# Forgetting heads' pages: keys turned on VectorE in 32x32 blocks, scores by token groups, values loaded in slices of 32 tokens

## The chip, the cores and the metric

One core of a Trainium2 chip runs the whole program. The metric is the device time in microseconds (us). PE is TensorE, DVE is VectorE, ACT is ScalarE, POOL is GpSimd and SP is SyncE, which issues DMAs. Everything is float32.

## The reference, cut to what matters

The kernel is one layer of a decoder. The change touches one part of it, the forgetting attention of the sample group: 8 sequences (b) of 8 new tokens each, 8 heads of 64 channels, and a paged cache of 2048 past tokens, 16 pages of 128 tokens for each sequence.

```
kv_past = cache_fox_kv[page_table]          # (8, 2048, 2, 8 heads, 64)
c  = cumsum(concat(logf_past, logf_new))    # forgetting: log decay up to each token
s  = q . k / 8  +  c_q  -  c_key            # (b, head, 8 queries, 2048 + 8 keys)
p  = softmax(where(key <= query, s, -inf))
o  = p . v
```

So 128 pages of keys and 128 pages of values (256 KB each) are read, keys must have their channels on the partitions for the score product, and weights must have their tokens there for the value product.

## The kernel before

Each engine has several Python generators ("streams"). Each yields a due time in the units of PLAN (line 143), and weave (line 158) puts the instructions of an engine's streams in the order of their due times. The order is fixed at build time; on the chip each engine takes its instructions in that order and waits on semaphores. The real time of a stretch is what its instructions take. PLAN's stage "fox", 869 to 1275, holds the pages of the forgetting heads. On PE it is interleaved with the gate projections of the prompt (gates_pe, lines 2246 and 2254), in units of 12 or 10 steps; a step is one 128-row product of 304 to 368 columns. A unit needs ScalarE's tanh of the unit before (line 2284) and VectorE's products (lines 2299 to 2305).

paged builds the schedule of the pages and pages_pe, pages_act, pages_dve play it, for this stage and two others. For the forgetting heads, four head pairs j side by side (rows 32j to 32j+16 of the score bank: 2 heads x 8 queries):

- T: a page of keys (128 tokens x 512) is transposed by PE in four 128x128 blocks into PSUM (line 1599), and copied to SBUF by ACT and DVE by turns (lines 1665, 1658). 128 pages.
- S: after each four pages, four products with 16 stationary columns and 512 moving ones (line 1615), one for each pair, side by side in the array. DVE adds the bias (the decay term) and takes the row maximum (line 1702). Group 4 is the 8 new tokens, against the new keys of all sequences (64 columns). Two score banks by turns.
- M: the maximum over the groups (line 1707), then ACT's exponential over 128 x 2112 elements with its row sum (line 1670).
- P: the weights are transposed by PE, four 128x128 blocks at a time, 17 in all (line 1624), and copied by DVE (line 1717).
- V: four parts, of four pages each (the last with the new tokens too), 16 products of 128 columns with 16 stationary ones to a part (line 1635). Then one scaling (line 1731), one transposition O (line 1642) and two copies (line 1735).

P, V and O of sequence b lie between the pages of b+1. Each of the 256 events has one place in the plan, with extra places after the last page.

Keys arrive through SP's queue (foxk_sp, line 1825) into a ring of 6 pages, which PE's transposition frees. Values arrive through ACT's queue (foxv_page_act, line 1858) into 8 places, freed four at a time by a V part. The bias rows are spread over the 16 rows of each pair by POOL's DMAs (foxbias_pool, line 1875), four for each group of four pages, 128 in all. foxprep makes these rows, from PSUM banks 3 to 6.

Of the kernel before, what the change touches and what calls it, by code (L numbers as in the profile page):

```python
# [22 lines left out]
P = 128  # L23
D = 1024
# [77 lines left out]
def make_sample_tables():  # L102

    new_f = np.full((P, NB, SM), NEG)
    pick = np.zeros((P, P))
    for j in range(4):
        for a in range(2):
            for t in range(NS):
                row = 32 * j + NS * a + t
                pick[2 * j + a, row] = 1  # L110
                for b in range(NB):
                    new_f[row, b, b * NS:b * NS + t + 1] = 0
    fox = np.concatenate([new_f.reshape(P, -1), pick], 1)
# [59 lines left out]
def build(nc, I, O, TAB):  # L173

    with ExitStack() as ctx:
# [1574 lines left out]
        NKR, NVR = 6, 8  # L1750
        SF = PAST + P
        s_fox = [take(SF, f0 + 1536 + SF * i) for i in range(2)]
        o_fox = take(P, f0 + 5888)
        stats_f = take(NB * (2 + 5), f0 + 6016)
        biasN = take(SM, f0 + 6080)
        vn_f = take(512, f0 + 6144)
        bias_f = take(1024, f0 + 6656).rearrange("p (g c) -> p g c", g=2)
        pages = [take(512, f0 + a) for a in (0, 512, 1024, 7680, 8192, 8704, 9216, 9728, 10240, 27680, 28192, 34848, 35360, 35872)]
        k_fox, v_fox = pages[0:NKR], pages[NKR:]
        PT_f = take((NPG + 1) * 64, f0 + 10752).rearrange("p (n j c) -> p n j c", j=4, c=16)  # L1760
        biasT = take(PAST, f0 + 11840)
        B_at = X0
        kts_f = [take(2048, a).rearrange("p (j c) -> p j c", j=4) for a in (f0 + 13888, B_at)]
# [3 lines left out]
        tab_f = take(NB * SM + P, C_at)  # L1767
        newadd = tab_f[:, 0:NB * SM].rearrange("p (b c) -> p b c", b=NB)
        pick_head = tab_f[0:HF, NB * SM:]
        ktn_f = take(4 * SM, C_at + 640).rearrange("p (j c) -> p j c", j=4)  # L1770
# [3 lines left out]
        page_in = ring([-(-(NB * NPG - i) // NKR) for i in range(NKR)] + [-(-(NB * NPG // 4 - i) // 3) * 4 for i in range(3)])  # L1774
# [3 lines left out]
        VP = 4  # L1778

# [49 lines left out]
        V_LAST, VK = NB * NPG - 8, 4  # L1829

        def v_place(n):

            if n < V_LAST:
                return v_fox[n % NVR], n - NVR
            if n < V_LAST + VK:
                return k_fox[n - V_LAST], None
            return v_fox[(n - VK) % NVR], n - VK - NVR

        def foxv_page_act(act):
            for n in range(NB * NPG):  # L1840
                if n == 0:
                    yield at("combine")(1) + 0.5
                    act.wait_ge(s_ptab, 16)
                place, before = v_place(n)
                if before is None:
                    yield pg_fox["due_of"][("T", NB - 1, NPG - 1)] + 0.4
                elif before >= 0:
                    yield pg_fox["due_of"][("V", before // NPG, before % NPG // 4)] + 0.1 + V_STEP * (before % 4)
# [3 lines left out]
                if before is None:  # L1852
                    act.wait_ge(*nth(pg_fox, "turned", NB * NPG))
                elif before >= 0:
                    act.wait_ge(*nth(pg_fox, "mixed", before // 4 + 1))
                else:
                    act.wait_ge(cb["second"], 4)
                act.dma_start(place, page_rows(pid, 1)).then_inc(fv_in[n // 4 % 3][0], 16)
# [5 lines left out]
        def foxbias_pool(pool):  # L1864
            pool.wait_ge(fb["rows_act"], 1)
            pool.wait_ge(fb["rows_dve"], 1)
            for q in range(4 * NB):
                b, G = q // 4, q % 4
                if q >= 2:
                    bb, GG = (q - 2) // 4, (q - 2) % 4  # L1870
                    pool.wait_ge(*nth(pg_fox, "drained", bb * 5 + 1 + GG))
                    pool.wait_ge(s_bias[q % 2], 64 * (q // 2))
                for j in range(4):
                    rows = biasT[b * HF + 2 * j:b * HF + 2 * j + 2, 512 * G:512 * (G + 1)]
                    pool.dma_start(bias_f[32 * j:32 * j + 16, q % 2, :],
                                   rows.unsqueeze(1).to_broadcast([2, NS, 512])).then_inc(s_bias[q % 2], 16)

        def fox_turns(b):
            return [dict(blocks=[k_fox[(b * NPG + p) % NKR][:, j * P:(j + 1) * P] for j in range(4)],
                         dst=lambda kt, p=p: kt[:, :, (p % 4) * P:(p % 4 + 1) * P],  # L1880
                         src=lambda bank: bank.rearrange("p (j c) -> p j c", j=4)) for p in range(NPG)]

        def fox_groups(b, kt):
            out = []
            for G in range(NPG // 4):
                mms = [] if kt is None else [(32 * j, 0, 512, qbF[:, j, b, :], kt[:, j, :], True, True) for j in range(4)]
                out.append(dict(turned=4 * (G + 1), first=True, mms=mms, drain=(G * 512, 512, bias_f[:, G % 2, :])))
            out.append(dict(turned=None, first=True, drain=(PAST, SM, newadd[:, b, :]),
                            mms=[(32 * j, 0, SM, qbF[:, j, b, :], ktn_f[:, j, :], True, True) for j in range(4)]))
            return out  # L1890

        def fox_pv(b):
            for p in range(NPG + 1):
                v = v_place(b * NPG + p)[0] if p < NPG else vn_f
                yield [(banks[7][32 * j:32 * j + 16, 0:P], PT_f[:, p, j, :], v[:, j * P:(j + 1) * P], p == 0, p == NPG)
                       for j in range(4)]

        def fox_p_keep(i, bank):
            n = min(4, NPG + 1 - 4 * i)
            v = bank[:, 0:n * P].rearrange("p (n j c) -> p n j c", j=4, c=32)  # L1900
            yield PT_f[:, 4 * i:4 * i + n, :, :], v[:, :, :, 0:16], None

        def fox_add_ready(eng, b, i):
            if i < 4:
                eng.wait_ge(s_bias[i % 2], 64 * ((4 * b + i) // 2 + 1))

        def fox_v_ready(eng, b, i):
            if b == 0 and i == VP - 1:
                eng.wait_ge(fb["vn_in"], 16)
                eng.wait_ge(fb["vn_clear"], 1)  # L1910
            q = b * VP + i
            landed(eng, fv_in[q % 3], 4 * (q // 3 + 1))

        fox_split = [list(range(4 * q, 4 * q + (4 if q < 3 else 5))) for q in range(VP)]
        fox_tail = [("V", q, 4 * (q + 1)) for q in range(VP)] + [("P", q, 2 + q) for q in range(5)] + [("O", 0, 17)]
        pg_fox = paged(fox_turns, fox_groups, P, kts_f, s_fox, NPG + 1, fox_p_keep, fox_pv, fox_split, o_fox, 1, stats_f,
                       pair_out(oTf, 4), fox_tail, PLAN["fox"],
                       dict(turn=banks[2:4], score=banks[4:6], tail=banks[6], o_ps=banks[7][:, 0:P]), add_ready=fox_add_ready, new_at=NPG - 1,
                       tail_step=1.0)

        def foxprep_pe(pe):
# [19 lines left out]
            pe.matmul(banks[7][:, 0:SM], pick_head, biasN[0:HF, :], start=True, stop=True).then_inc(fb["new_spread"], 1)  # L1941

        def foxprep_act(act):
# [3 lines left out]
            act.activation(biasT[0:SM, 1024:2048], psum[0:SM, 5 * 512:7 * 512], ACT.Copy).then_inc(fb["rows_act"], 1)  # L1947
# [32 lines left out]
        def foxprep_dve(dve):  # L1980
# [3 lines left out]
            dve.memset(bias_f, 0.0)  # L1984
            dve.wait_ge(fb["summed"], 1)
            dve.tensor_copy(biasN[0:HF, :], banks[7][0:HF, 0:SM]).then_inc(fb["new_kept"], 1)
            dve.tensor_copy(biasT[0:SM, 0:1024], psum[0:SM, 3 * 512:5 * 512]).then_inc(fb["rows_dve"], 1)
# [6 lines left out]
            dve.tensor_tensor(newadd, newadd, banks[7][:, 0:SM].unsqueeze(1).to_broadcast([P, NB, SM]),  # L1994
                              ALU.add).then_inc(fb["cleared"], 1)

        def foxpages_pe(pe):
# [5 lines left out]
            yield from pages_pe(pe, pg_fox, lambda e, b, i: landed(e, fk_in[(b * NPG + i) % NKR], (b * NPG + i) // NKR + 1),  # L2003
                                fox_v_ready)

        def foxpages_act(act):
            yield PLAN["fox"][0]
            act.wait_ge(cb["second"], 4)
            yield from pages_act(act, pg_fox)

        def foxpages_dve(dve):
            yield PLAN["fox"][0]
            for i in range(2):
                dve.memset(s_fox[i][:, PAST + SM:], 0.0)
            dve.memset(vn_f[SM:P, :], 0.0).then_inc(fb["vn_clear"], 1)
            dve.wait_ge(fb["cleared"], 1)
            yield from pages_dve(dve, pg_fox)
# [10 lines left out]
        k_dil = [take(DPG * 256, a).rearrange("p (n c) -> p n c", n=DPG) for a in (f0 + 11840, f0 + 7424)]  # L2028
# [1646 lines left out]
```

## Time and profile before

| | before |
|---|---|
| median of 3 runs, us | 2620.23 (2615.91 to 2621.1) |
| the profiled execution, us | 2616.37 |
| its span, us | 2614.6 |
| PE busy | 2576.3 us (99%) |
| DVE, ACT, POOL busy | 1240.2 (47%), 515.1 (20%), 178.6 us (7%) |
| DMA | 299.24 MB, mean 114 GB/s |
| first to last key page on PE | 787 to 1060 us |

The profile is of one execution. Rows that begin with a line number and an engine are groups of instructions: line, engine, operation, output<-input with shapes, xcount, then busy us, mean ns of one, and idle time before them with what ended it. PEld is the weight load of a product, which overlaps PE. A float32 product is two records of PE; a transposition is one. Rows of the timeline begin with the start in us and the length in us; consecutive instructions of a line are merged into one row, with their count.

### The profile page before, as it was taken

The numbers are of one execution on the slowest core, as the hardware profiler recorded it, in microseconds if no ns is written. First come the engines' busy times: TensorE is split into PE (matmuls) and PEld (weight loads), VectorE is DVE, ScalarE is ACT, GpSimd is POOL, SyncE is SP. The second block draws the span as 40 slices with busy tenths as digits, with TensorE's granted clock in tenths as the row PEclk, the third lists the DMA queues.
The fourth block names the chain that finished last, engine by engine and source line by source line (L and its number), as shares of the span: only waits on it lengthen the run. The fifth ranks groups of instructions, "written<-read, shape, count | busy, mean of one in ns | idle before, by whom it ended". The sixth has DMA issues, their size and how long they took to land.

```text
span 2614.6 us, 38053 instructions
## 1 busy us (share of the span) xinstructions
PE 2576.3 (99%) x14402; PEld 1833.6 (70%) x14402; DVE 1240.2 (47%) x2999; ACT 515.1 (20%) x1127; POOL 178.6 (7%) x284
## 2 busy tenths in 40 slices
PE   8999999999999999999999999999999999999999
PEld 7766566666656666676445885558888888888887
DVE  2577553333253333353553443356666666644432
ACT  2233223222202222121011112311121212110002
POOL 1000002132202222000000000000000000000000
PEclk9999999999999999999999999999999999999999
DMA  5000202201118888786215004434543542163201
GB/s 199 16 11 12 64 4 63 64 20 38 31 39 258 249 268 266 229 272 221 101 49 213 33 18 149 152 82 137 176 144 124 164 148 68 33 203 94 67 31 69
DMA packets 208476, 299.24 MB, mean 114 GB/s; under 512 B 20941, under 2 KB 145246, under 8 KB 207254
## 3 DMA queue, kind: packets, MB, share of 16 engines
q1 hardware_dynamic: 149462, 192.47, 22.8%
q10 hardware_dynamic: 42976, 89.26, 10.6%
q0 software_dynamic: 15856, 15.07, 2.3%
q8 instruction: 116, 1.90, 0.3%
q14 instruction: 66, 0.54, 0.1%
HBM read 270.43 MB, written 65.71 MB: 129 GB/s over the span
## 4 chain that ended last, share of the span: by engine, by line
PE 95%; DMA 2%; DVE 1%; ACTq 1%; issue 1%; ACT 0%; SPq 0%; DVEq 0%
PE psum L3051 22%; PE psum L3433 11%; PE psum L1240 10%; PE psum L2246 8%; PE psum L2334 4%; PE psum L629 4%; PE psum L2733 4%; PE psum L1599 3%; PE psum L2435 3%; PE psum L2254 3%; PE psum L873 3%; PE psum L890 2%; PE psum L2711 2%; PE psum L1615 2%; PE psum L1635 2%; PE psum L901 1%
## 5 line engine op out<-in xcount | busy, mean ns | idle before, releaser
L3051 PE MATMUL psum<-arena 128*128 128x272 f32 x2464 | 568.0, 394 | 1.2 <-DVE arena L3125 1.2
L3051 PEld LDWEIGHTS psum<-arena 128*128 128x128 f32 x2464 | 470.0, 191 | 98.6 <-issue 1.3
L1240 PE MATMUL psum<-arena 128*128 128x512 f32 (+3 forms) x960 | 286.4, 460 | 3.4 <-DVE arena L738 3.4
L3433 PE MATMUL psum<-arena 128*128 128x256 f32 (+1 forms) x1584 | 288.1, 356 | 0.0
L2246 PE MATMUL psum<-arena 128*128 128x368 f32 (+1 forms) x768 | 279.1, 475 | 1.2 <-DVE arena L2182 0.6
L3433 PEld LDWEIGHTS psum<-arena 128*128 128x128 f32 (+1 forms) x1584 | 252.4, 178 | 34.7 <-issue 3.2
L1240 PEld LDWEIGHTS psum<-arena 128*128 128x128 f32 (+1 forms) x960 | 150.8, 180 | 93.6 <-issue 82.9
L3154 DVE TENSOR_TENSOR arena<-arena,psum 128x272 f32<-128x272 f32 (+2 forms) x330 | 111.6, 377 | 112.9 <-PE psum L3051 112.1
L2246 PEld LDWEIGHTS psum<-arena 128*128 128x128 f32 x768 | 127.8, 190 | 52.3 <-issue 14.8
L1599 PEld LDWEIGHTS psum<-arena 128*128 128x128 f32 x848 | 105.1, 141 | 69.2 <-issue 45.8
L3175 DVE SCALAR_TENSOR_TENSOR arena<-arena 128x1024 f32<-128x1024 f32 x88 | 113.1, 1285 | 52.6 <-ACT arena L3077 51.1
L1658 DVE COPY arena<-psum 128x512 f32<-128x512 f32 (+1 forms) x108 | 73.6, 681 | 128.1 <-PE psum L1599 127.9
L3075 ACT ACTIVATE arena<-arena 128x1024 f32<-128x1024 f32 x44 | 54.3, 1233 | 401.3 <-DVE arena L3154 401.3
L3545 DVE TENSOR_TENSOR arena<-arena,psum 128x256 f32<-128x256 f32 (+1 forms) x128 | 46.6, 401 | 178.9 <-PE psum L3433 178.8
L1599 PE MATMUL psum<-arena 128*128 128x128 f32 x848 | 127.4, 273 | 3.3 <-DMA arena<-in_cache_fox_kv 1.7
L2334 PE MATMUL psum<-arena 128*128 128x512 f32 x256 | 122.0, 596 | 0.0
L1665 ACT ACTIVATE arena<-psum 128x512 f32<-128x512 f32 (+1 forms) x108 | 63.6, 589 | 294.1 <-PE psum L1599 287.0
L629 PE MATMUL psum<-arena 128*128 128x272 f32 x448 | 117.4, 400 | 0.0
L2733 PE MATMUL psum<-arena 128*128 128x272 f32 x448 | 108.2, 392 | 0.0
L2254 PE MATMUL psum<-arena 128*128 128x352 f32 (+2 forms) x288 | 100.8, 457 | 0.0
L2435 PE MATMUL psum<-arena 128*128 128x512 f32 x224 | 98.0, 593 | 0.8 <-issue 0.8
L629 PEld LDWEIGHTS psum<-arena 128*128 128x128 f32 x448 | 79.6, 190 | 24.7 <-issue 12.1
(285 smaller groups left out, 2988.0 us busy)
## 6 DMA issues: line engine op xcount, KB each, us to landing
arena<-in_cache_fox_kv ACTq DMA_DIRECT2D x128, 256.0 KB, 4.7
arena<-in_cache_fox_kv SPq DMA_DIRECT2D x128, 256.0 KB, 5.0
out_win_s<-in_cache_win_kv ACTq DMA_DIRECT2D x8, 4080.0 KB, 15.1
arena<-in_w_up SPq DMA_DIRECT2D x44, 512.0 KB, 6.4
arena<-in_w_down SPq DMA_DIRECT2D x14, 1408.0 KB, 6.5
arena<-in_cache_win_kv SPq DMA_DIRECT2D x16, 1024.0 KB, 8.1
arena<-in_cache_mem_kv SPq DMA_DIRECT2D x16, 1024.0 KB, 6.2
out_y_p<-arena SPq DMA_DIRECT2D x20, 512.0 KB, 2.7
```

The source lines that it names most:

```text
L629: last = pe.matmul(banks[q % 3][:, 0:QT4], w, r, start=(k == 0), stop=(k == 3))
L1240: last = pe.matmul(banks[c0 // 512][p0:p0 + r, 0:n], xn_tile(k, g, t), wD[g][:, k, w0:w0 + n], start=(k == 0), stop=(k == KD - 1))
L1599: last = pe.transpose(a["turn"][n % 2][:, x * P:(x + 1) * P], k, ident)
L2246: last = pe.matmul(banks[0][:, 0:cw], w[:, k, :], xnT[:, k, c0:c0 + cw], start=(k == 0), stop=(k == KD - 1))
L2254: last = pe.matmul(banks[1][:, 0:pw], w[:, 8 + k, :], oT[:, k, c0:c0 + pw], start=(k == 0), stop=(k == kn - 1))
L2334: last = pe.matmul(banks[h], lhs(k)[:, t * P:(t + 1) * P], w[h][:, k, :], start=(k == 0), stop=(k == KD - 1))
L2435: last = pe.matmul(mix_out(u), merged[:, ks, tok + t * P:tok + (t + 1) * P][:, k, :], wm[side][:, ws, :][:, k, :], start=(k == 0), stop=(k ...
L2733: last = pe.matmul(query_bank(n), w[:, k, :], r[:, k, XT4 * p:XT4 * p + XT4], start=(k == 0), stop=(k == 3))
L3051: last = pe.matmul(bank_of(j, x, p), w[:, k, :], r[:, k, Q4 * p:Q4 * p + Q4], start=(k == 0), stop=(k == 3))
L3154: last = dve.tensor_tensor(dst, dst if base is None else view(base), view(bank), ALU.add)
L3175: dve.scalar_tensor_tensor(out=tp, in0=up[:, tap:tap + S], scalar=w, in1=tp, op0=ALU.mult, op1=ALU.add).then_inc(done, 1)
L3433: last = pe.matmul(down_out(u)[p0:p0 + r, 0:n], hT(f)[:, tok + t * P:tok + t * P + r], slot[slots[c]][:, f - fa, c0:c0 + n], start=(f == f ...
```

## The change

Only the forgetting heads' pages and what prepares them change; PLAN does not.

- **T** is on DVE: one instruction transposes a key page (128 x 512) in its 32x32 blocks, SBUF to SBUF. Block (i, x) of the result holds channels 32x to 32x+31 on partitions 32i.. for tokens 32i to 32i+31. So on the partitions lie 4 token groups i times 32 channels, and the free axis has 16 channel blocks x by 32 tokens of each group. PE has no key transposition, and ACT and DVE have no copies of them.
- **S**: q_blocks (made by DVE, 16 small copies for each sequence: event W) holds the queries on the diagonal of the token groups, so that 32 stationary columns (4 token groups x 8 queries) times 128 moving columns (4 pages x 32 tokens) give the scores of one head; two channel blocks are summed. 16 products for each four pages instead of 4, into banks 2 (head a=0 of each pair) and 3 (a=1), which stay full until all 16 pages are scored.
- **D** and **M** come once for each sequence: two additions with maximum of 512 columns, two of 8 for the new tokens (DN), then the maximum over token groups by two 32x32 transpositions, a reduction and a copy between them. ACT has four exponentials (two of 512 columns, two of 8).
- **P** has 10 transpositions in three batches instead of 17 in five; **L** is a new product that adds the sums of the token groups.
- **V** has the same count of products; its rows are now tokens 32i+c of a page on partition c of a slice, so a value page is loaded into 32 partitions as 4 rows of 2 KB each, and four pages lie below each other on the 128 partitions.
- Rings: keys 5 pages (before 6); values 3 places of four pages (before 8 single pages).
- The bias rows: 64 DMAs of 32 rows instead of 128 of 16; foxprep's two copies of 1024 columns become eight of 256 columns on each of ACT and DVE, from 32 partitions.

The times of events: SLOTS = 146 equal parts of the stage, a page per slot; S at 4.5 slots after the first page of its group, D 16.6, M 16.7, W 17.2, P 18.2, 19.2, 20.2, L 21.2, V 20.2, 24.2, 28.2, 32.2 and O 33.4 slots after the first page of the sequence.

```diff
-            for q in range(4 * NB):
...
-                rows = biasT[b * HF + 2 * j:b * HF + 2 * j + 2, 512 * G:512 * (G + 1)]
+            for b in range(NB):
+                for a in range(2):
+                    if b:
+                        pool.wait_ge(*nth(pg_fox, "drained", 4 * b - 1 + a))
+                        pool.wait_ge(s_bias[a], 64 * b)
+                    for j in range(4):
...
+        fox_events = [(n, "T", n // NPG, n % NPG) for n in range(NB * NPG)]
+        for b in range(NB):
+            fox_events += [(NPG * b + 4 * G + 4.5, "S", b, G) for G in range(4)]
+            fox_events += [(NPG * b + 5.5, "N", b, 0), (NPG * b + 6.0, "DN", b, 0), (NPG * b + 16.6, "D", b, 0),
+                           (NPG * b + 16.7, "M", b, 0), (NPG * b + 17.2, "W", b, 0)]
+            fox_events += [(NPG * (b + 1) + 2.2 + q, "P", b, q) for q in range(3)]
+            fox_events += [(NPG * (b + 1) + 5.2, "L", b, 0), (NPG * (b + 1) + 17.4, "O", b, 0)]
+            fox_events += [(NPG * (b + 1) + 4 * (q + 1) + 0.2, "V", b, q) for q in range(VP)]
...
+                rows = slice(32 * (n % 4), 32 * (n % 4) + 32)
+                act.dma_start(v_place(g)[rows, :, :], page_rows(pid, 1).rearrange("(i c) f -> c i f", i=4)
...
         def foxpages_pe(pe):
...
+                if what == "S":
+                    if i == 0:
+                        pe.wait_ge(*nth(pg_fox, "made", b + 1))
+                        if b:
+                            pe.wait_ge(*nth(pg_fox, "drained", 4 * b))
+                    pe.wait_ge(*nth(pg_fox, "turned", NPG * b + 4 * i + 4))
+                    kt = kts_f[i % 2]
+                    for a in range(2):
+                        for x in range(2):
+                            for j in range(4):
+                                last = pe.matmul(banks[2 + a][32 * j:32 * j + 32, P * i:P * (i + 1)],
+                                                 q_blocks[b % 2][:, j, 2 * a + x, :, :], kt[:, 4 * j + 2 * a + x, :],
+                                                 start=(x == 0), stop=(x == 1))
...
+                elif what == "P":
+                    if i == 0:
+                        pe.wait_ge(*nth(pg_fox, "expd", 4 * (b + 1)))
+                        if b:
+                            pe.wait_ge(*nth(pg_fox, "taken", b))
...
         def foxpages_act(act):
...
+                yield fox_due["M", b, 0]
+                act.wait_ge(*nth(pg_fox, "maxed", 5 * (b + 1)))
+                if b:
+                    act.wait_ge(s_fox_sums, b)
+                for x in range(4):
...
+                    act.activation(p, p, ACT.Exp, bias=low_f[:, a:a + 1], accum_out=sum_f[:, x:x + 1]
...
+        def fox_query_blocks(dve, b):
+
+            for x in range(4):
+                for i in range(4):
+                    last = dve.tensor_copy(q_blocks[b % 2][32 * i:32 * i + 32, :, x, i, :],
+                                           qbF[32 * x:32 * x + 32, :, b, NS * (x // 2):NS * (x // 2 + 1)])
+            last.then_inc(pg_fox["s"]["made"], 1)
...
+                if what == "T":
+                    n = NPG * b + i
+                    landed(dve, fk_in[n % NKR], n // NKR + 1)
+                    if n >= 8:
+                        dve.wait_ge(*nth(pg_fox, "scored", scores_of(*divmod(n // 4 - 2, 4))))
+                    dve.transpose(kts_f[i // 4 % 2][:, :, 32 * (i % 4):32 * (i % 4) + 32],
+                                  k_fox[n % NKR].rearrange("p (x c) -> p x c", c=32)).then_inc(s["turned"], 1)
...
+                elif what == "M":
+                    dve.wait_ge(*nth(pg_fox, "drained", 4 * (b + 1)))
+                    dve.tensor_tensor(top_f[:, 0:2], max_f[:, 0:2], max_f[:, 2:4], ALU.max).then_inc(s["maxed"], 1)
...
+                    dve.transpose(low_f, low_fT).then_inc(s["maxed"], 1)
+                elif what == "W" and b + 2 < NB:
+                    fox_query_blocks(dve, b + 2)
...
+                elif what == "O":
+                    dve.wait_ge(*nth(pg_fox, "o_turned", b + 1))
+                    for dst, src in pair_out(oTf, 4)(b, banks[6]):
+                        last = dve.tensor_copy(dst, src)
+                    last.then_inc(s["taken"], 1)
```

## Rows read from the trace of the kernel before

**Rows 1.** The page, part 1: busy time of each engine
```profile
PE 2576.3 (99%) x14402; PEld 1833.6 (70%) x14402; DVE 1240.2 (47%) x2999; ACT 515.1 (20%) x1127; POOL 178.6 (7%) x284
```

**Rows 2.** The page, part 4: the chain that ended last, by engine
```profile
PE 95%; DMA 2%; DVE 1%; ACTq 1%; issue 1%; ACT 0%; SPq 0%; DVEq 0%
```

**Rows 3.** Stretches from:to and length, busy by engine, PEclk, DMA share, GB/s
```profile
787.00:797.00 10.00, 8.69 (x47) 4.91 (x48) 2.33 (x5) 1.79 (x3) 0.05 (x1) 1.00 1.06 365
787.00:1060.00 273.00, 268.98 (x2258) 174.66 (x2259) 96.82 (x231) 60.52 (x102) 66.36 (x120) 1.00 0.87 258
```

**Rows 4.** Groups of instructions from 787 to 1060 us
```profile
L2246 PE MATMUL psum<-arena 128*128 128x368 f32 x224 | 86.4, 479 | 0.0
L1599 PE MATMUL psum<-arena 128*128 128x128 f32 x492 | 74.1, 273 | 3.2 <-DMA arena<-in_cache_fox_kv 1.7 <-ACT arena L1665 1.5
...
L1658 DVE COPY arena<-psum 128x512 f32<-128x512 f32 x61 | 42.2, 691 | 73.8 <-PE psum L1599 73.8
L2246 PE MATMUL psum<-arena 128*128 128x352 f32 x112 | 41.5, 468 | 0.0
L1665 ACT ACTIVATE arena<-psum 128x512 f32<-128x512 f32 x62 | 37.0, 598 | 170.5 <-PE psum L1599 163.4 <-issue 3.9 <-PE psum L1615 3.2
...
L2254 PE MATMUL psum<-arena 128*128 128x368 f32 x44 | 16.9, 478 | 0.0
L2254 PE MATMUL psum<-arena 128*128 128x352 f32 x44 | 16.2, 467 | 0.0
...
L2254 PE MATMUL psum<-arena 128*128 128x304 f32 x41 | 14.1, 428 | 0.0
```

**Rows 5.** Timeline of PE: a page, a gate step, an S group, a V part
```profile
930.42 0.60 PE L1599 MATMUL psum<-arena 128*128 128x128 f32 x4
930.85 0.78 PE L2246 MATMUL psum<-arena 128*128 128x368 f32 x2
931.47 0.60 PE L1624 MATMUL psum<-arena 128*128 128x128 f32 x4
...
933.68 1.05 PE L1615 MATMUL psum<-arena 128*16 128x512 f32 x8
934.55 1.05 PE L1635 MATMUL psum<-arena 128*16 128x128 f32 x32
935.54 1.50 PE L2246 MATMUL psum<-arena 128*128 128x368 f32 x4
```

**Rows 6.** Timeline of PE: three V parts in one burst, and what follows
```profile
1086.89 3.03 PE L1635 MATMUL psum<-arena 128*16 128x128 f32 x104
1089.85 2.12 PE L2246 MATMUL psum<-arena 128*128 128x368 f32 x6
```

**Rows 7.** Timeline, all engines: from the last scores to the exponential
```profile
958.58 1.16 PE L1615 MATMUL psum<-arena 128*16 128x512 f32 x16
...
959.70 0.69 DVE L1702 CUSTOM_DVE_ANT_0 arena<-psum,arena 128x512 f32<-128x512 f32 x1 [1.95 <-PE psum L1615]
...
960.58 0.16 DVE L1707 TENSOR_REDUCE arena<-arena 128x1 f32<-128x5 f32 x1
...
960.93 2.06 ACT L1670 ACTIVATE arena<-arena 128x2112 f32<-128x2112 f32 x1 [0.53 <-PE psum L1635]
...
962.90 0.19 ACT L1670 ACTIVATION_READ_ACCUMULATOR arena<-arena 128x1 f32 x1
```

**Rows 8.** Groups of DVE over the whole span: SBUF to SBUF
```profile
L3140 DVE TENSOR_TENSOR arena<-arena 128x512 f32<-128x512 f32 x22 | 15.2, 693 | 0.8
...
L3164 DVE COPY arena<-arena 128x16 f32<-128x16 f32 x44 | 7.7, 176 | 1.5
```

**Rows 9.** DMA, 787 to 1060 us: queues (packets, MB, share), key loads (us to landing)
```profile
q10 hardware_dynamic: 25229, 32.79, 39.4%
q1 hardware_dynamic: 18293, 33.23, 38.1%
...
arena<-in_cache_fox_kv SPq DMA_DIRECT2D x123, 256.0 KB, 4.9
```

More of the change, by code:

```diff
@@ L102, in make_sample_tables @@
 def make_sample_tables():
-    new_f = np.full((P, NB, SM), NEG)
-    pick = np.zeros((P, P))
+    new_f = np.full((P, 2, SM), NEG)
+    pick = np.zeros((P, 2, P))
+    over = np.zeros((P, P))
+    own = np.zeros((P, 2, 2))
     for j in range(4):
-        for a in range(2):
+        for i in range(4):
             for t in range(NS):
[L109 to L113, printed above, removed]
+                row = 32 * j + NS * i + t
+                for a in range(2):
+                    pick[2 * j + a, a, row] = 1
+                over[row, 32 * j + t:32 * j + 32:NS] = 1
+                own[row, :, i % 2] = 1
+                if i == 0:
+                    for b in range(NB):
+                        new_f[row, :, b * NS:b * NS + t + 1] = 0
+    fox = np.concatenate([new_f.reshape(P, -1), pick.reshape(P, -1), over, own.reshape(P, -1)], 1)
     m = np.full((P, DWID), NEG)
@@ L1773, in build @@
         s_bias = [sem(f"fox_bias_rows_spread{g}") for g in range(2)]
-        page_in = ring([-(-(NB * NPG - i) // NKR) for i in range(NKR)] + [-(-(NB * NPG // 4 - i) // 3) * 4 for i in range(3)])
+        page_in = ring([-(-(NB * NPG - i) // NKR) for i in range(NKR)] + [-(-(NB * NPG // 4 - 1 - i) // NVG) * 4 for i in range(NVG)] + [4])
+        s_fox_sums = sem("fox_weights_summed")
         fk_in, fv_in = page_in[0:NKR], page_in[NKR:]
@@ L1878, in fox_turns @@
[L1878 to L1915, printed above, removed]
@@ new lines, in build @@
+        fox_events.sort(key=lambda e: (e[0], e[2]))
+        fox_totals = dict(turned=NB * NPG, kept_even=0, kept_odd=0, scored=5 * NB, drained=4 * NB, maxed=5 * NB, expd=4 * NB,
+                          p_turned=3 * NB, p_kept=3 * NB, inverted=3 * NB, mixed=VP * NB)
+        fox_s, fox_z = again("pages", "turned kept_even kept_odd scored drained maxed expd p_turned p_kept inverted "
+                             "mixed scaled o_turned taken made", lambda n: fox_totals.get(n, NB))
+        fox_due = {e[1:]: PLAN["fox"][0] + (PLAN["fox"][1] - PLAN["fox"][0]) * e[0] / SLOTS for e in fox_events}
@@ L1940, in foxprep_pe, with bias_rows @@
             pe.wait_ge(fb["new_kept"], 1)
-            pe.matmul(banks[7][:, 0:SM], pick_head, biasN[0:HF, :], start=True, stop=True).then_inc(fb["new_spread"], 1)
+            for a in range(2):
+                last = pe.matmul(banks[7][:, SM * a:SM * (a + 1)], pick_head[:, a, :], biasN[0:HF, :], start=True, stop=True)
+            last.then_inc(fb["new_spread"], 1)
+        def bias_rows(half):
+            src = psum[0:SM, (3 + 2 * half) * 512:(5 + 2 * half) * 512].rearrange("r (p i c) -> r p i c", i=4, c=32)
+            for b in range(2):
+                for i in range(4):
+                    yield (biasR[32 * i:32 * i + 32, b, 256 * half:256 * half + 256].rearrange("r (p c) -> r p c", c=32),
+                           src[32 * b:32 * b + 32, :, i, :])
         def foxprep_act(act):
@@ L1946, in foxprep_act @@
             act.wait_ge(fb["summed"], 1)
-            act.activation(biasT[0:SM, 1024:2048], psum[0:SM, 5 * 512:7 * 512], ACT.Copy).then_inc(fb["rows_act"], 1)
+            for dst, src in bias_rows(1):
+                last = act.activation(dst, src, ACT.Copy)
+            last.then_inc(fb["rows_act"], 1)
         def lf_turn_at(n):
```

220 lines of the change are left out of this document (163 added, 57 removed).

## The prediction

> **What bounds the kernel now.** I read the busy shares first: PE is busy 99% of the span, DVE 47%, ACT 20% [rows 1]. The chain that ended last lies on PE for 95% [rows 2]. So microseconds of work taken from PE are gained, as long as nothing else becomes late. Then the windows: the stretch of the key pages, 787 to 1060 us, has PE at 268.98 of 273 us, at the full granted clock (1.00, 2.4 GHz), DVE at 96.82 and DMA at a share of 0.87 with 258 GB/s [rows 3]. That is what the reader is to see: in this stretch DMA is close behind PE. The timeline gives what each step costs PE, from start to next start, which is not its length (lengths overlap).
>
> **PE's work, part by part.**
> - Key transpositions: four take 930.85 - 930.42 = 0.43 us [rows 5]; 128 pages x 0.43 = 55 us go. It checks: a gate step behind them takes 931.47 - 930.85 = 0.62 us [rows 5] and is not lengthened by them.
> - P: 7 of 17 transpositions of a sequence go, 56 x 0.43/4 = 6 us.
> - S: a group takes 934.55 - 933.68 = 0.87 us before [rows 5]. After, it has 16 products, 32 records of 128 columns, four side by side. Their nearest row is V: 104 records in 1089.85 - 1086.89 = 2.96 us, 28.5 ns each [rows 6], and a part of 32 takes 935.54 - 934.55 = 0.99 us with the change-over [rows 5], so that change-over is 0.99 - 32 x 0.0285 = 0.08 us. 0.91 us of records instead of 0.87: +1 us over 32 groups. Weights of 32 columns instead of 16 are in no row; between these 28.5 ns and the 108 ns of a 128-column one (0.43/4) I take the near end, since four still lie side by side; at 40 ns it would be +12 us.
> - S and V stood back to back. Now 0.3 slots lie between them, 0.8 units of plan, where a gate step comes every 1.5 (15.2 units to 10 steps), so in about half the cases a step is put between and two change-overs more are paid: 16 to 32 x 0.17, +3 to +5 us; I take 3.
> - The new tokens: their score group cost 1.16 - 1.05 = 0.11 us behind the last S [rows 5, 7]; now 16 records on their own, 0.46 + 0.17: +4 us over 8. L: +1 us.
> - Sum: -55 - 6 + 1 + 3 + 4 + 1 = -52 us of PE work. V and O have the same instructions.
>
> **What is late next: the softmax of each sequence.** Before, the maximum was taken along with the groups. After the last scores, DVE began at 959.70, 1.12 us after PE began them at 958.58, had the total maximum by 960.74, and ACT's exponential ran 960.93 to 963.09 [rows 7]. P came some pages later. Now both banks are drained only after all 16 pages, and the chain runs, counted from PE's start on the last S:
> - DVE's first D starts at 1.0 + 0.25 = 1.25 us; two of 512 columns at 0.70 each (0.69 [rows 7]): 2.65.
> - M: five small dependent operations, 0.16 [rows 7] plus 0.04 between: 3.65.
> - ACT: 0.19 to start [rows 7]. 512 columns take 0.60 [rows 4] and 2112 take 2.06, so a column 0.9 ns and a tiny operation 0.13; the read of a sum adds 0.19 [rows 7], of which 0.1 lies beside the operation. Two of 512 columns and two tiny ones: 2 x 0.75 + 2 x 0.3 = 2.1. Done at 5.95.
> - DVE meanwhile has in its queue the next T (0.69 by the 512-column row [rows 8]), then W, 16 copies at 0.17 [rows 8] = 2.7 to 2.8 us, then O's two copies, about 0.2 each by the same row, and the first P of PE waits for that O ("taken"): 3.65 + 0.69 + 2.75 + 0.4 = 7.5 us.
>
> PE has in front of that P: S itself 1.0, change-overs and O 0.3, and the gate steps of 1.7 slots. A slot is 406/146 = 2.78 units; 1.7 slots are 4.7 units, 3.1 steps, 1.95 us. Cover 3.3 us. So PE stands 7.5 - 3.3 = 4.2 us for the sequences 1 to 5, which have W and O, and 5.95 - 3.3 = 2.7 us for 0, 6 and 7: 21 + 8 = 29 us. Bounds: 15 us if the small operations cost half, 45 if gate operations of DVE and ACT, some 0.5 us each (368 columns lie between the rows of 16 and of 512 [rows 8]), stand in the chain as well. The second and third P have a slot each, 0.43 + 1.2 us, against 0.5 + 0.9 for transposing and copying two times 256 columns: covered.
>
> **The other edits.**
> - DVE loses 61 copies (42.2 us [rows 4]) and 16 additions of 0.69 (11 us [rows 7]); it gains 128 transpositions and 128 small copies (22 us). A DVE transposition is in no row of before. Below it stands the small copy, 0.17 us, above it nothing; the nearest row is 512 columns from SBUF to SBUF, 0.69 [rows 8]. I take 0.69: 88 us. DVE goes from 97 to 154 us in a stretch of about 250: hidden. It becomes the bound only from about (250 - 66)/128 = 1.4 us each.
> - ACT loses its copies: off the path.
> - Bias rows: half as many DMAs of twice the rows, with 16 slots between the drain that frees a bank's rows and the next use: hidden. foxprep: eight copies of 256 columns (0.43 each by the slope of [rows 8], 3.4 us) for one of 1024 (1.2 by the same), on each engine, and two sets of query blocks at the start (5.5 us on DVE), while PE has gate steps and the first keys are in flight until 787: +1 us, up to 6 if that cover is gone.
> - Key ring 5 instead of 6: five slots are over 9 us ahead; hidden while a load lands in 4.9 us [rows 9].
>
> **DMA.** The stretch keeps its gate steps: 465 records [rows 4], 232 steps. Before, T(7,15) stood at place 243 or so of 274, 360 units; after at 128 x 2.78 = 356. So its PE work is 269 - 52 = 217 us at least, with the softmax waits 246. The stretch moved 0.87 x 273 = 237 us worth of DMA [rows 3]. That leaves 9 us of slack in 246. It reached 365 GB/s at a share of 1.06 in its first 10 us [rows 3], so 237 is not a hard floor, but keys and values come in bursts, and before, at 0.87, PE already lost a few us to them (1.7 us at L1599 [rows 4]). I take 10 us of waits for pages, 0 to 25, against 3 before: +7.
>
> **The sum.** Own execution 2616.4 - 52 + 29 + 1 + 7 = 2601. The median is 3.9 above that execution (2620.2 to 2616.4), so 2605.
>
> **A rule that speaks against it.** The stretch is at 0.87 of DMA: q1 (keys) moves 33.23 MB in 38.1% and q10 (values and gate weights) 32.79 MB in 39.4% of it [rows 3, 9], 319 and 305 GB/s while they run. No row of before has a large load into 32 partitions. The Trainium skill, in "SBUF — State Buffer", section "Door 1: The DMA port swizzle", says that partitions 0 to 31 reach only 8 of 16 ports and measured 189 GB/s there, against 328 on all; an estimate from that page is 1.4 to 1.7 times the time for each value page. It is the third rival, which is priced without it.
>
> **The rivals.**
> 1. *The chain is covered* (15%). DVE and ACT get ahead because small operations are quicker than their rows, and PE saves its whole 52 us less 10. For it: DVE is idle half of the time. Against: the order is fixed, and D cannot start before the last S. DMA then sets the stretch, at about 237/0.98 = 242 us, 25 above PE's 217 where 4 were idle before: 2616.4 - 52 + 1 + 21 = 2586, with the median's 3.9: 2590. If DMA keeps up too, with 10 us of waits, 2575.
> 2. *The query-block copies and ACT's order cost more* (10%): chain at its upper bound of 45 us: 2621, no change.
> 3. *Slower: the value slices load at half width* (22%). A page that lands on 32 partitions keeps fewer ways into memory busy, so q10's time for values grows. Place: q10, where the values of seven sequences less the eight pages loaded ahead, 104 x 256 KB, are 27.3 of 32.8 MB: 0.394 x 273 x 27.3/32.8 = 89.5 us [rows 9]. With a factor f on it, the stretch needs 237 + 89.5(f - 1) us of DMA. It binds above 256 us, from f = 1.2. It makes the kernel slower from a stretch of 272 us, f = 1.4. At f = 1.5 the stretch is 282 + 5: own 2601 + 31 = 2632, median 2636. At 2 it is 327 + 5: 2681. For it: DMA is the second bound here and the values are two fifths of it. Against: keys run beside them on all partitions, and neighbouring slices take other partitions.
> 4. *DVE's transposition costs 1.4 us or more* (5%): DVE is the bound; at 2 us, 66 + 256 = 322 us, 66 more than the forecast's 256: 2671. The Trainium skill, in "VectorE: DVE Perf Modes", "The three transpose paths", gives 311 ns for 128x128 in bf16; no row here shows one, and by it four would be an estimate of about 1 us, still under cover.
>
> **How the numbers follow.** My forecast, 2605, has 48%; its own range is 2588 to 2619, from the bounds of the chain (15 to 45), of PE's work (-40 to -56) and of the waits for pages. The range that holds 8 in 10 takes in rival 1 down to 2578 and rival 3 up to f = 1.5: 2578 to 2636. A change under 0.2%, 5 us, can't be told from none here. Faster than 2615: most of the forecast (42 of 48), rival 1 (15), part of 3 at small f (6): 63%. Same: 14%. Slower: 23%.
>
> **What would show it.** Right: no L1599 records on PE before the next stage, 512 fewer records; S groups of about 0.9 us; idle time of PE before the first P transposition of each sequence, 2.7 to 4.2 us, eight times, released by DVE's O copies or ACT's exponential; DMA share from 0.93 up in a stretch of about 250 us. Wrong: this idle time absent (rival 1); PE waiting on values, q10 with far more time for the same MB, loads landing well above 4.9 us (rival 3); DVE busy near 100% (rival 4); S groups over 1.3 us (weights of 32 columns cost more). If the stretch is short but the time the same, the gain was given back later, where the window pages of the next stage follow.

## The result: slower, 2639.85 us

| | before | after |
|---|---|---|
| median, us | 2620.36 (4 runs) | 2639.85 (2635.92 to 2642.13, 4 runs) |
| ratio after/before | | 1.0075, 95% interval 1.0059 to 1.009 |
| span of the profiled execution, us | 2614.6 | 2638.9 |
| PE busy, us | 2576.3 | 2548.5 |
| first to last key page, us | 787 to 1060 | 790 to 1088 |

I had forecast 2605 with a range of 2578 to 2636. The page of the changed kernel, parts 1 and 4, which answer to [rows 1, 2]:

```profile
PE 2548.5 (97%) x14684; PEld 1811.3 (69%) x14684; DVE 1303.1 (49%) x3233; ACT 478.5 (18%) x1118; POOL 144.7 (5%) x220
...
PE 90%; DMA 4%; ACTq 3%; DVE 2%; issue 1%; ACT 0%; SPq 0%; DVEq 0%
```

PE is busy 28 us less and the span is 24 us longer: PE stands idle 90.4 us (2638.9 - 2548.5) instead of 38.3. The chain shows DMA with 4% and ACT's queue with 3%. The stretch of the key pages, with the columns of [rows 3], then its first 10 us, then the parts around one sequence's softmax:

```profile
787.00:1085.00 298.00, 247.41 (x2642) 157.07 (x2640) 156.00 (x439) 24.38 (x84) 32.18 (x56) 0.92 1.05 244
787.00:797.00 10.00, 7.23 (x52) 4.52 (x51) 6.43 (x22) 0.00 (x0) 0.00 (x0) 0.94 1.06 245
...
937.00:941.00 4.00, 0.23 (x1) 0.01 (x1) 3.72 (x20) 2.09 (x8) 3.10 (x6) 1.00 1.04 275
941.00:946.00 5.00, 4.75 (x15) 2.96 (x16) 3.37 (x7) 0.48 (x1) 0.00 (x0) 0.66 1.09 260
946.00:952.00 6.00, 6.00 (x94) 3.72 (x94) 2.64 (x8) 0.00 (x0) 0.00 (x0) 1.00 1.07 225
```

Before, a DMA share of 0.87 carried 258 GB/s. Now 1.05 carries 244. In the first 10 us, at the same share of 1.06, 365 GB/s have become 245 [rows 3]: DMA is as busy as it was and moves less. DVE is where I had it, 156 us (154 forecast). The queues from 787 to 1060 us, which answer to [rows 9], and the loads' time from issue to landing:

```profile
q10 hardware_dynamic: 24568, 31.58, 51.2%
q1 hardware_dynamic: 17028, 31.05, 45.6%
...
arena<-in_cache_fox_kv SPq DMA_DIRECT2D x117, 256.0 KB, 9.4
arena<-in_cache_fox_kv ACTq DMA_DIRECT2D x103, 256.0 KB, 10.7
```

Values and gate weights take 0.512 x 273/31.58 = 4.43 us per MB instead of 0.394 x 273/32.79 = 3.28. The keys, whose loads were not changed, take 4.01 instead of 3.13. A key page lands in 9.4 us instead of 4.9.

Who waits for that, in the stretch (waiter <- releaser: us in total, times, longest):

```profile
PE psum L2400 <- ACT arena L2438: 18.4, 5, 7.3
PE psum L2040 <- DVE arena L2170: 13.3, 3, 5.4
PE psum L2017 <- DVE arena L2110: 6.9, 6, 2.8
PE psum L2040 <- ACT arena L2078: 6.8, 3, 3.5
PE psum L2060 <- DMA arena<-in_cache_fox_kv: 3.2, 2, 2.5
...
DVE arena L2110 <- DMA arena<-in_cache_fox_kv: 82.1, 60, 4.2
```

On PE, L2040 are the weight transpositions (P), L2017 the scores, L2060 the value products and L2400 the gates. On DVE, L2110 are the key transpositions and L2170 O's copies; on ACT, L2078 is the exponential and L2438 the gates' tanh. DVE waits for keys 60 times; PE sees only part of that by name. The largest wait, gates for ACT's tanh, goes back to DMA too, as the first experiment will show. ACT also issues the value loads and the gate weights. One issue of a value load now holds its queue up to 5.9 us (1.9 before), one of gate weights up to 8.8 us (2.2 before), and the tanh behind comes late: issues of gate weights of 8.3 and 8.8 us, with value loads behind them, stand ahead of the two longest waits, 5.2 and 7.3 us.

The softmax chain is as it was forecast. Timeline of the changed kernel, last scores of sequence 3 to its first P (L2126 is D, L2142 the end of M, L2085 the query-block copies W, L2408 gates as well):

```profile
933.39 1.06 PE L2017 MATMUL psum<-arena 128*32 128x128 f32 x32
934.38 1.50 PE L2400 MATMUL psum<-arena 128*128 128x368 f32 x4
934.51 0.69 DVE L2126 CUSTOM_DVE_ANT_0 arena<-psum,arena 128x512 f32<-128x512 f32 x1 [0.46 <-PE psum L2017]
936.76 0.21 DVE L2142 STREAM_TRANSPOSE arena<-arena 128x32 f32<-128x32 f32 x1
937.49 2.97 DVE L2085 COPY arena<-arena 32x32 f32<-32x32 f32 x16
938.91 0.18 ACT L2078 ACTIVATION_READ_ACCUMULATOR arena<-arena 128x1 f32 x1
940.49 0.39 DVE L2170 COPY arena<-psum 64x32 f32<-64x32 f32 x2
941.02 0.63 PE L2040 MATMUL psum<-arena 128*128 128x128 f32 x4 [3.80 <-DVE arena L2170]
943.34 1.43 PE L2400 MATMUL psum<-arena 128*128 128x368 f32 x2
944.57 1.43 PE L2408 MATMUL psum<-arena 128*128 128x368 f32 x2
```

From 933.39 to 941.02 is 7.6 us (7.5 forecast), with 3.80 us of idle time (4.2 forecast), released by O's copies behind the 16 query-block copies. What I had not counted stands in the last two rows: a gate step takes 944.57 - 943.34 = 1.23 us instead of 0.62. The granted clock, 1.00 from 930 to 941, is 0.66 on average over 941 to 946: part of it at the lower level, 1.2 GHz, behind the idle time of 3.80 us.

### The profile page after: what moved, and what is told of

It reads as the page before. It is cut to its first block, busy times and chain, and to the rows that moved or that the text cites. A ratio compares the mean times of both kernels' runs of the same rounds, so it can differ in the third digit from the quotient of the medians.

```text
span 2638.9 us, 38565 instructions
## 1 busy us (share of the span) xinstructions
PE 2548.5 (97%) x14684; PEld 1811.3 (69%) x14684; DVE 1303.1 (49%) x3233; ACT 478.5 (18%) x1118; POOL 144.7 (5%) x220
## 4 chain that ended last, share of the span: by engine, by line
PE 90%; DMA 4%; ACTq 3%; DVE 2%; issue 1%; ACT 0%; SPq 0%; DVEq 0%
PE psum L3205 21%; PE psum L3587 11%; PE psum L1246 10%; PE psum L2400 7%; PE psum L2488 4%; PE psum L635 4%; PE psum L2887 4%; PE psum L2589 3%; PE psum L879 3%; PE psum L896 2%; DMA arena<-in_cache_fox_kv 2%; PE psum L2408 2%; PE psum L2865 2%; PE psum L907 1%; PE psum L1605 1%; PE psum L443 1%
## 5 line engine op out<-in xcount | busy, mean ns | idle before, releaser
L3205 PEld LDWEIGHTS psum<-arena 128*128 128x128 f32 x2464 | 469.7, 191 | 98.1 <-issue 0.9
L2400 PE MATMUL psum<-arena 128*128 128x368 f32 (+1 forms) x768 | 280.9, 496 | 19.1 <-ACT arena L2438 18.4
L2400 PEld LDWEIGHTS psum<-arena 128*128 128x128 f32 x768 | 140.0, 198 | 93.7 <-ACT arena L2438 20.8
L2110 DVE STREAM_TRANSPOSE arena<-arena 128x512 f32<-128x512 f32 x128 | 90.0, 706 | 89.5 <-DMA arena<-in_cache_fox_kv 87.6
L2408 PE MATMUL psum<-arena 128*128 128x352 f32 (+2 forms) x288 | 101.2, 471 | 0.0
L635 PEld LDWEIGHTS psum<-arena 128*128 128x128 f32 x448 | 79.6, 190 | 24.7 <-issue 12.1
L2887 PEld LDWEIGHTS psum<-arena 128*128 128x128 f32 x448 | 84.2, 190 | 16.0
L930 ACT ACTIVATE arena<-arena 128x256 f32<-128x256 f32 (+7 forms) x96 | 65.3, 680 | 152.6 <-DVE arena L956 151.3
L956 DVE CUSTOM_DVE_ANT_0 arena<-psum,arena 128x512 f32<-128x512 f32 (+3 forms) x128 | 65.2, 537 | 53.9 <-PE psum L879 53.4
```

Of the source, the lines that this page charges most:

```text
L635: last = pe.matmul(banks[q % 3][:, 0:QT4], w, r, start=(k == 0), stop=(k == 3))
L2110: dve.transpose(kts_f[i // 4 % 2][:, :, 32 * (i % 4):32 * (i % 4) + 32], k_fox[n % NKR].rearrange("p (x c) -> p x c", c=32)).then_inc(s["t ...
L2400: last = pe.matmul(banks[0][:, 0:cw], w[:, k, :], xnT[:, k, c0:c0 + cw], start=(k == 0), stop=(k == KD - 1))
L2408: last = pe.matmul(banks[1][:, 0:pw], w[:, 8 + k, :], oT[:, k, c0:c0 + pw], start=(k == 0), stop=(k == kn - 1))
L2887: last = pe.matmul(query_bank(n), w[:, k, :], r[:, k, XT4 * p:XT4 * p + XT4], start=(k == 0), stop=(k == 3))
L3205: last = pe.matmul(bank_of(j, x, p), w[:, k, :], r[:, k, Q4 * p:Q4 * p + Q4], start=(k == 0), stop=(k == 3))
```

## The experiments

Theory A: value pages that land on 32 adjoining partitions make all of DMA slower, and DMA sets the stretch. Rival B: the softmax waits and the clock behind them are the loss, and DMA is full only because requests queue up.

The kernel before was run again with each group of experiments, with medians of 2618 to 2620 us; the ratios are to that median, differences in us between experiments are of their medians. The kernels with whole-width loads, a quarter of the values, or slices in the kernel before leave value tokens in the wrong order or out, as their texts say; the others leave nothing out.

**Whole-width loads in the changed kernel.**

```diff
-                rows = slice(32 * (n % 4), 32 * (n % 4) + 32)
-                act.dma_start(v_place(g)[rows, :, :], page_rows(pid, 1).rearrange("(i c) f -> c i f", i=4)
+                act.dma_start(v_place(g)[:, n % 4, :], page_rows(pid, 1)
```

> The changed kernel, but each value page is loaded into all 128 partitions (one row of 2 KB each, beside each other in the group's place) instead of into a slice of 32. Same bytes, same 128 rows, same semaphores; the value product then meets the tokens in the wrong order, so the output for the sample group is not the reference's. Theory A (the slices load slowly, and that fills DMA): q10's time per MB goes back to about before's (3.3 us per MB instead of 4.4), the DMA share in the key stretch falls from 1.07 to about 0.95, pages land in 5 to 6 us instead of 10, the stretch from 298 to 255-265 us, the whole to 2598-2606 us. Rival B (the softmax waits and the clock that falls behind them make the loss, DMA is full only because requests queue up): DMA time per MB stays, the whole stays within 5 us of 2640.

Measured: 2609.09 us (ratio to before 0.9962, 0.9949 to 0.9975), 31 below after and 3 above the range that A gave. Line numbers are one lower here (L2039 for L2040). Queues and key loads from 787 to 1060 us, then PE's waits:

```profile
q10 hardware_dynamic: 28259, 36.58, 41.3%
q1 hardware_dynamic: 19247, 34.15, 38.1%
...
arena<-in_cache_fox_kv SPq DMA_DIRECT2D x124, 256.0 KB, 5.0
...
PE psum L2039 <- DVE arena L2169: 17.1, 4, 4.5
PE psum L2039 <- ACT arena L2077: 8.2, 3, 3.0
PE psum L2399 <- ACT arena L2437: 3.6, 1, 3.6
```

q10 takes 3.08 us per MB, and the keys are back to 3.05. B falls as the whole story. The waits at P stay, 17.1 + 8.2 us, and the wait for the tanh falls from 18.4 to 3.6 us with nothing of ACT edited but the shape of its value loads, whose longest issue is 1.0 us.

**The other way round: slices in the kernel before.** 124 of 128 value pages go to 32 partitions each; the rings' places were moved to make groups of four.

```diff
+                    place = v_groups[m // 4 % 2][32 * (n % 4):32 * (n % 4) + 32, :, :]
+                    src = src.rearrange("(i c) f -> c i f", i=4)
```

> The kernel before, with nothing changed but the value loads: each page goes into 32 partitions as four rows (124 of 128 pages; the four that go to key places stay whole). Tokens then stand in the wrong order for the value product, so the output for the sample group is not the reference's. Theory A: DMA needs about 283 us for what it did in 237, so the stretch from first to last key page grows from 273 to 285-295 us and the whole to 2632-2645 us, with a share over 1.0. Rival B: 2620, as before, since nothing of the softmax is changed.

Measured: 2682.14 us (1.0244, 1.0222 to 1.0267). The direction is A's, the size is 37 us above A's upper bound: 62 us from one load's shape, with the softmax of before. The expectation counted DMA's time and left out the clock: with the same 14402 records, PE is busy 2598.1 us instead of 2576.3, 22 us of the loss.

```profile
787.00:1060.00 273.00, 241.63 (x1931) 152.54 (x1930) 82.33 (x196) 52.01 (x87) 55.19 (x100) 0.96 1.01 220
...
q10 hardware_dynamic: 21447, 27.65, 48.1%
q1 hardware_dynamic: 15722, 28.67, 44.1%
...
PE psum L1635 <- DMA arena<-in_cache_fox_kv: 16.8, 6, 7.3
PE psum L1599 <- ACT arena L1665: 14.1, 4, 5.7
PE psum L1599 <- DMA arena<-in_cache_fox_kv: 8.0, 9, 1.6
```

q10 and q1 take 4.75 and 4.20 us per MB.

**Is it 32 partitions, or that they adjoin?** Page n goes to partitions n%4, n%4+4, ...: same bytes, rows and count of partitions. The bias columns, not shown, are put in the same order.

```diff
-                rows = slice(32 * (n % 4), 32 * (n % 4) + 32)
+                rows = slice(n % 4, P, 4)
...
-                    dve.transpose(kts_f[i // 4 % 2][:, :, 32 * (i % 4):32 * (i % 4) + 32],
+                    dve.transpose(kts_f[i // 4 % 2][:, :, i % 4:P:4],
```

> The changed kernel, with the 32 partitions of a value page spread over the memory: page n goes to partitions n%4, n%4+4, ..., (step 4) instead of to 32 adjoining ones; the key transposition writes its columns with step 4 and the bias columns are put in the same order, so that the result is the reference's. Bytes, rows and rows per DMA engine are the same. Theory A in the form 'adjoining partitions share ways into memory': as with whole-width loads, 2598-2606 us. Theory A in the form '32 partitions are too few, wherever they lie': as after, 2640. Rival B: 2640. A cost may hide it: if DVE's transposition with step 4 takes over 1.2 us instead of 0.71, DVE becomes late.

Measured: 2615.06 us (0.9982, 0.9969 to 0.9994), 25 below after, 9 above the range for this form of A and far from the 2640 of the others. It is that they adjoin:

```profile
q10 hardware_dynamic: 27720, 35.94, 40.3%
q1 hardware_dynamic: 18717, 33.69, 36.7%
...
L2110 DVE STREAM_TRANSPOSE arena<-arena 128x512 f32<-128x512 f32 x128 | 132.7, 1097 | 12.5 <-DMA arena<-in_cache_fox_kv 12.2
```

q10 takes 3.06 us per MB, with 32 partitions. The Trainium skill, in "SBUF — State Buffer", "Door 1: The DMA port swizzle", takes the port from bits 2 to 4 and 6 of the partition's number: 32 adjoining partitions have 8 of 16 ports, every fourth partition has all. The runs agree with that table; they do not show ports themselves. Two prices are seen: a transposition that writes with a step takes 1.10 instead of 0.71 us, and ACT's queue takes 0.61 us to issue a spread value load (median), against 0.33 for an adjoining slice and 0.34 for a whole-width load.

The same slices in the kernel before (`v_groups[...][n % 4:P:4, :, :]`):

> The kernel before with the value pages in slices of 32 partitions as in e2_before_sliced, but page n on partitions n%4, n%4+4, ... (step 4) instead of adjoining ones; not the reference's output for the sample group. If what makes slices slow is that adjoining partitions share ways into memory, this runs like before: 2618-2624 us, q10 at about 3.3 us per MB. If a load of 4 rows to each of 32 partitions is slow by itself, it runs like e2_before_sliced: 2680.

Measured: 2624.44 us (1.0025, 1.0011 to 1.0039), q10 at 0.391 x 273/32.49 = 3.29 us per MB. It leaves the range by 0.4 us and is a fourth of a per cent above before, against 2.4% for adjoining slices; the moved rings are the same in both, so they are not the 2.4%. What the last 6 us are was not tried; PE's waits for ACT's copies of the keys go from 1.5 to 4.1 us, and here too an issue of ACT's takes 0.61 us.

**A quarter of the value bytes** (`v_place(g)[rows, 0:1, :]`), so that DMA is no bound.

> The changed kernel with a quarter of the value bytes: each value page's load brings 32 rows of 2 KB instead of 128 (one of the four rows of each partition); the rest of the place keeps what was there, so the output for the sample group is not the reference's. This takes DMA off as a bound and leaves the softmax waits alone. Both theories agree on the waits (2.7 to 4.2 us before each sequence's first weight transposition, about 29 us, and a lowered clock behind each); it measures them: stretch 248-258 us, whole 2592-2602 us. If the whole is well below, at 2575 or less, the softmax waits were no loss of their own.

Measured: 2607.08 us (0.9954, 0.9941 to 0.9968), a miss by 5 us on the high side. The DMA share is 0.70 and PE still waits 17.8 + 8.2 us at P; the granted clock is 0.94. So with DMA out of the way 2607 is left, and whole-width loads were at 2609. That the second cost is the softmax chain with its clock is argued up to here; the next runs try it.

**A cheaper way to spread.** The value slices stay spread. The key transposition writes together; the score product reads its moving columns with a step.

```diff
-                                                 q_blocks[b % 2][:, j, 2 * a + x, :, :], kt[:, 4 * j + 2 * a + x, :],
+                                                 q_blocks[b % 2][:, j, 2 * a + x, :, :],
+                                                 kt[:, 4 * j + 2 * a + x, :].rearrange("r (p c) -> r c p", p=4),
```

> As e3_spread (value page n on partitions n%4, n%4+4, ...), but the key transposition writes its blocks together again (0.71 us instead of 1.10) and the score product reads its moving columns with a step instead; the bias columns are in the same order as there. The result is the reference's. If the 0.39 us more for each key page was what kept e3_spread 6 us above the kernel with whole-width loads, this gives 2607-2611 us. If a moving operand read with a step slows PE, the S groups take more than 1.0 us (at 2 us each: +32 us, 2640).

Measured: 2643.98 us (1.0098, 1.0081 to 1.0115), the bad end of what was expected. A group of scores, then what follows it, on PE (L2401 for L2400):

```profile
934.26 2.07 PE L2017 MATMUL psum<-arena 128*32 128x128 f32 x32
936.27 1.50 PE L2401 MATMUL psum<-arena 128*128 128x368 f32 x4
```

A group takes 936.27 - 934.26 = 2.01 us instead of 934.38 - 933.39 = 0.99: 32 x 1.02 = 33 us of PE. So this run can't tell what the transposition with a step had cost.

**The softmax chain, on that kernel.** First W at slot 22.0 instead of 17.2.

> e5_spread_cheap, with the 16 query-block copies (event W) at slot 22.0 instead of 17.2, so that they no longer stand ahead of O's copies in VectorE's queue, which PE's first weight transposition waits for. By the theory of the softmax chain, PE's wait falls from 4.5 to about 2.9 us in the five sequences 1 to 5, then released by ScalarE's exponential: 8 us less idle time, and a little less of the lowered clock: 2597-2603 us. Rival (those waits are slack that is paid elsewhere anyway): within 3 us of e5.

Measured: 2635.25 us, 8.7 below e5_spread_cheap. The step is of the expected size, 8, but the range of 2597 to 2603 was missed by 32: it was written for a base without the slow scores. PE's waits at P go from 17.3 us behind O's copies and 5.6 behind the exponential to 15.1 behind the exponential alone. Then P, L, V and O 2.2 slots later:

> e6_blocks_later, with P, L, V and O 2.2 slots later (P at 20.4 instead of 18.2 slots), which puts 4 more gate steps, 2.5 us, between the last scores and the first weight transposition. By the theory the remaining waits of 2.7 us are gone, and the granted clock in the stretch goes back from 0.95 to 0.99 or 1.00; then PE's saved work shows whole, less what DMA takes back: 2570-2588 us. Rival (the clock is low for another reason, such as the small products): the waits go but the clock stays at 0.95: 2588-2595. Third (DMA takes it all back, share over 1.0 again): above 2595.

Measured: 2613.07 us (0.9982, 0.9972 to 0.9992), another 22 less, and again above its range (2570 to 2588), by 25, for the same reason. The stretch in e6_blocks_later, then here:

```profile
787.00:1060.00 273.00, 250.60 (x2422) 160.60 (x2420) 145.91 (x425) 24.00 (x83) 32.09 (x56) 0.96 0.82 254
787.00:1060.00 273.00, 264.87 (x2633) 166.04 (x2633) 154.09 (x443) 24.50 (x84) 32.09 (x56) 0.99 0.88 269
```

The waits at P are gone and the stretch's clock is 0.99 with the same small products: the clock came back when the idle times went. 15 us of waits gave 22; with the same 14684 records, PE's busy time in the whole kernel fell from 2573.2 to 2564.2 us.

**The same two moves on the changed kernel, slices adjoining:**

> The changed kernel with adjoining slices as it is, and only the two moves of events of e6 and e7 (W at 22.0, P, L, V and O 2.2 slots later). If slow value slices set the stretch alone, this takes PE's waits at P away and they come back as waits for pages: 2630-2642 us, DMA share still 1.05 or more. If the two costs add, it gains as much as e7 does over e5: 2610 us or less.

Measured: 2632.45 us (1.0058, 1.0041 to 1.0074): 7 less than after (4 to 5 by the ratios to before), where the same moves gave 31 with spread slices. The DMA share is still 1.05:

```profile
PE psum L2017 <- DVE arena L2110: 22.3, 14, 3.4
PE psum L2400 <- ACT arena L2438: 18.2, 5, 8.2
```

The waits moved from P to the key pages (22.3 us instead of 6.9). The two costs do not add; the adjoining slices hid most of the other.

**Both mended.** e3_spread with the two moves, and whole-width loads with them:

> e3_spread (value slices on every fourth partition, the key transposition writing with a step, 1.10 us) with the two moves of events of e7_weights_later (W at 22.0, P, L, V and O 2.2 slots later). The result is the reference's. If the two costs found so far (adjoining slices; PE waiting at P and the lowered clock behind it) are all that is between the forecast and PE's saved work, the kernel comes to 2616 - 52 + 5 to 15 = 2570 to 2582 us, faster than both. If VectorE's 133 us of transpositions makes it late at the score groups, or DMA's share goes above 1.0: 2585-2600.

> e1_full_width (whole-width value loads, tokens out of order, so not the reference's output for the sample group) with the same moves of events. It has the cheap key transposition (0.70 us) and the fast loads at once: the lower end of what this plan of work can do. 2565-2580 us, and 0 to 6 us below e9_spread_later; the distance is what the transposition with a step costs.

Measured: 2585.46 us (0.9869, 0.9849 to 0.9889) and 2578.86 (0.9843, 0.9823 to 0.9863). The first leaves nothing out and is the fastest version that does not, 1.3% below before and 2.1% below after. It missed the upper bound of its main case by 3 us and lies at the edge of its second case, DVE late at the scores. Its stretch:

```profile
787.00:1030.00 243.00, 228.96 (x2574) 143.20 (x2576) 198.08 (x446) 25.06 (x86) 32.21 (x56) 0.99 0.95 298
...
PE psum L2017 <- DVE arena L2110: 6.3, 7, 1.8
PE psum L2400 <- ACT arena L2438: 5.7, 6, 1.6
```

The stretch takes 243 us instead of 273, PE is busy 229 of them, and DMA moves 298 GB/s. The page of e10_full_width_later, part 1, shows PE's work without the waits:

```profile
PE 2533.0 (98%) x14684; PEld 1800.5 (70%) x14684; DVE 1300.5 (50%) x3233; ACT 479.2 (19%) x1118; POOL 144.7 (6%) x220
```

6.6 us lie between the two. The transposition with a step is at most a part of it: PE's waits for L2110 are 6.3 us against 4.1, but those for ACT's tanh are 5.7 against 2.1, and ACT issues the spread loads slower. How the 6.6 us divide was not tried.

## Why the prediction was wrong

- *The account.* The forecast was 52 us of work off PE and 37 us of idle time more. The changed kernel has 52 us more of idle time (90.4 against 38.3) and only 28 less of busy time.
- *PE's work, -52 us.* Nearly right. Where the clock is at 0.99 again, PE is busy 2533.0 us in both mended kernels, 43 less than the 2576.3 of [rows 1]; where the other 9 us are was not looked into. S groups were priced at 0.91 + 0.08, measured 0.99: weights of 32 columns cost nothing more.
- *The softmax chain, +29 us.* Right in its place, its order and its size: 3.80 us against 4.2 in the sequence shown, and 26 us in all with whole-width loads (17.1 + 8.2 + 0.5). Left out was the clock behind each wait: 15 us of waits were worth 22 in e7_weights_later, and the changed kernel's PE is busy 15.5 us longer than the mended kernels' with the same records (2548.5 against 2533.0).
- *DVE's transposition,* taken as 0.69 from [rows 8]: 0.705. Rivals 1, 2 and 4 did not come.
- *DMA, +7 us: this step failed.* I took the stretch's 237 us worth of DMA as fixed by its bytes and asked only whether it fits, though the change gives half of these bytes another shape of destination. It needed 1.05 x 298 = 313 us, and the stretch took 301 (787 to 1088) instead of 256. With the loads' shape alone set back, the kernel ran at 2609: the shape is 31 us there, and 62 in the kernel before. That 2609 is so near to the forecast of 2605 is in part luck: that kernel has 29 us more of idle time than before, not 37 (2605.1 - 2537.9 = 67.2 against 38.3), and 38 less of busy time, not 52.
- *Rival 3* is what happened, at 22%, and its price was short: I put the factor on the values' 89.5 us only. The keys share the 16 DMA engines with them and went from 3.13 to 4.01 us per MB. "Against: keys run beside them on all partitions" was the wrong way round: they were slowed, not a help. That its 2636 is near the 2639.85 is luck. It stands for f = 1.5; with the measured 4.43/3.28 = 1.35 the same sum gives a stretch of 237 + 31 + 5 = 273 us and a median of 2622. The factor set too high made up for the keys and the clock, which it left out.
- The rule of the Trainium skill stood in the text with an estimate of 1.4 to 1.7 times for a value page. The 4.43 us per MB, gate weights included, are 1.35 times the 3.28 of before, a little under it, and the measurement decides. That page, in the Trainium skill "SBUF — State Buffer", "Door 1: The DMA port swizzle", puts such a load at half of the ports. The chance I gave it was too low, for no row of before spoke against it.

## What to carry to other kernels

Bytes do not price a DMA: when a change alters which partitions a load fills, its time per MB is unknown until a row of the same shape is seen. Here, where DMA was at 0.87 before, the other loads paid as well (keys 3.13 to 4.01 us per MB). Slices of 32 partitions can be spread (every fourth one) instead of adjoining, if something cheap can permute the columns to match. And a wait of PE can cost more than its length (here 15 us gave 22), so after moving work off PE, place what depends on a long chain at least that chain's length later in the order.

## What the runs showed of the hardware that I had not expected

- 32 adjoining partitions as destination: 4.3 to 4.8 us per MB for the queue with these loads and 3.9 to 4.2 for whole-width ones beside them (after, e2_before_sliced, e8_after_weights_later); every fourth partition: 3.1 to 3.3 and 3.0 (e3_spread, e9_spread_later, e11_before_spread). An issue on ScalarE's queue takes 0.33 us for an adjoining slice and 0.61 us for a spread one.
- PE reading a float32 moving operand with a step of 32 elements takes 2.01 us for 32 records instead of 0.99. DVE's transposition of 128x512 in 32x32 blocks takes 1.10 instead of 0.71 us when it writes with a step of 4.
- With adjoining slices and a DMA share of 1.05, one issue instruction on ScalarE's queue lasted up to 5.9 us for a value page and 8.8 us for gate weights (1.9 and 2.2 before); ScalarE's tanh behind them came late, and PE waited 18.4 us for it, 3.6 with whole-width loads.
- Behind an idle time of PE of 3.8 us the granted clock was 0.66 over the next 5 us (after, 941 to 946); without such waits it was 0.99 over the whole stretch, with the same small products (e7_weights_later).
